# Memory is transposed un-normed, with its root applied at keys and values; its two weight slots are cut in pieces

## The reference

```python
mem_kv = (rms_norm(mem, mem_norm) @ w_mem_kv).reshape(B, M, 2, MEM_HEADS, MEM_HEAD_DIM)
mem_k, mem_v = mem_kv[:, :, 0], mem_kv[:, :, 1]
u = rms_norm(h, even_norm1[j])
q, k, v, qm = jnp.split(u @ even_w_in[j], [NA_WIDTH, 2 * NA_WIDTH, 3 * NA_WIDTH], axis=-1)
```

## Time and profile before

| what | value |
|---|---|
| median of 3 runs | 1448.41 us (1445.82 to 1448.61) |
| profiled execution, its own time | 1446.34 us |
| span of the profiled execution | 1444.1 us |
| PE busy | 1408.7 us, 98% |
| DVE busy | 1156.4 us, 80% |
| ACT busy | 974.7 us, 67% |
| mean transfer rate | 302 GB/s |

### The profile page before, as it was taken

The page is one execution under the profiler, slowest core; times in us unless marked ns, Lnnn a source line. Parts: engine busy times, 40 slices in busy tenths (PEclk is TensorE's granted clock), DMA queues, the critical chain, the costliest instruction groups (busy, mean ns, idle before and its releaser), DMA issues.

```text
span 1444.1 us, 19732 instructions
## 1 busy us (share of the span) xinstructions
PE 1408.7 (98%) x7228; PEld 1184.3 (82%) x7228; DVE 1156.4 (80%) x1013; ACT 974.7 (67%) x929; POOL 69.7 (5%) x70
## 2 busy tenths in 40 slices
PE   6999999998999999999999999999999999999997
PEld 6997888887977788888888888888888888888885
DVE  5567756664674888988888899889888889888887
ACT  6455645444853577777777777787777777777775
POOL 0000100000010300100000000000010000000000
PEclk9999999999999999999999999999999999999999
DMA  8634455544454899999999999999999999999992
GB/s 263 218 127 146 152 199 203 177 142 133 137 176 150 299 368 387 355 393 393 374 369 394 386 360 393 386 354 396 395 372 375 393 377 368 396 383 357 393 361 74
DMA packets 201942, 435.88 MB, mean 302 GB/s; under 512 B 10959, under 2 KB 41251, under 8 KB 201892
## 3 DMA queue, kind: packets, MB, share of 16 engines
q1 hardware_dynamic: 198836, 424.70, 81.1%
q0 software_dynamic: 3056, 10.50, 2.5%
HBM read 427.30 MB, written 7.88 MB: 301 GB/s over the span
## 4 chain that ended last, share of the span: by engine, by line
PE 93%; DVE 3%; ACT 2%; issue 1%; DMA 1%; POOL 0%; SPq 0%; DVEq 0%; POOLq 0%; ACTq 0%
PE ps L1583 26%; PE ps L1585 26%; PE ps L1584 26%; PE ps L1865 5%; PE ps L1867 3%; PE ps L2142 2%; DVE w_lo L1003 1%; ACT w_hi L547 1%; DMA raw<-mem_kv 1%; PE ps L1708 0%; PE ps L1672 0%; PE ps L2052 0%; PE ps L2164 0%; PE ps L1999 0%; PE ps L1686 0%
## 5 line engine op out<-in xcount | busy, mean ns | idle before, releaser
L1471 DVE TENSOR_TENSOR w_lo<-raw,w_hi 128x2048 fp32r<-128x2048 f32 (+1 forms) x221 | 436.0, 1981 | 57.0 <-ACT w_hi L847 56.7
L847 ACT ACTIVATE w_hi<-raw 128x2048 fp32r<-128x2048 f32 (+1 forms) x221 | 367.4, 1669 | 119.7 <-PE ps L1585 119.7
L1583 PE MATMUL ps<-w_hi,xt_both 128*128 128x512 f32 (+2 forms) x1048 | 405.8, 387 | 3.3 <-DVE xt_both L1364 1.5
L1585 PE MATMUL ps<-w_hi,xt_both 128*128 128x512 f32 (+2 forms) x1048 | 400.0, 382 | 0.0
L1584 PE MATMUL ps<-w_lo,xt_both 128*128 128x512 f32 (+2 forms) x1048 | 399.4, 381 | 0.0
L1471 DVE TENSOR_TENSOR w_lo<-arena,w_hi 128x2048 fp32r<-128x2048 f32 x144 | 294.8, 2052 | 27.0 <-ACT w_hi L847 26.8
L847 ACT ACTIVATE w_hi<-arena 128x2048 fp32r<-128x2048 f32 x144 | 248.8, 1728 | 82.4 <-PE ps L1585 82.4
L1583 PEld LDWEIGHTS ps<-w_hi,xt_both 128*128 128x128 f32 x1048 | 197.0, 188 | 41.1 <-issue 4.7
L1585 PEld LDWEIGHTS ps<-w_hi,xt_both 128*128 128x128 f32 x1048 | 196.9, 188 | 37.4
L1584 PEld LDWEIGHTS ps<-w_lo,xt_both 128*128 128x128 f32 x1048 | 197.2, 188 | 35.0
L1583 PE MATMUL ps<-w_hi,hT_hi 128*128 128x512 f32 x560 | 219.4, 392 | 0.0
(11 more groups left out here) (266 smaller groups left out, 1223.0 us busy)
## 6 DMA issues: line engine op xcount, KB each, us to landing
raw<-exp_gate SPq DMA_DIRECT2D x72, 1024.0 KB, 7.6
raw<-exp_up SPq DMA_DIRECT2D x48, 1024.0 KB, 8.8
arena<-exp_down SPq DMA_DIRECT2D x48, 1024.0 KB, 6.7
arena<-exp_up SPq DMA_DIRECT2D x40, 1024.0 KB, 8.4
raw<-exp_down SPq DMA_DIRECT2D x40, 1024.0 KB, 8.3
arena<-exp_gate SPq DMA_DIRECT2D x24, 1024.0 KB, 8.5
raw<-exp_up SPq DMA_DIRECT2D x32, 512.0 KB, 6.0
raw<-even_gate SPq DMA_DIRECT2D x11, 1024.0 KB, 5.3
```

What stands on the lines that cost most here:

```text
L847: ins = act.activation(w_hi[:, n % CUT, at:at + src.shape[1]], src, ACT.Copy)
L1471: ins = dve.tensor_tensor(w_lo[:, n % CUT, cols], src, w_hi[:, n % CUT, cols].bitcast(F32), ALU.subtract)
L1583: pe.matmul(dst, a[0], b[0], start=start, stop=False, skip_group_check=shared)
L1585: return pe.matmul(dst, a[1], b[0], start=False, stop=stop, skip_group_check=shared)
```

## The change

- Memory is no longer normed before its transposes: PE transposes it as it lands. Its squares are taken by ACT after x has been turned, its epsilon and root follow later (POOL takes the roots of x first; `NORM_STEP` gives the order of counts).
- The inverse root of each memory row goes to the results: values (rows on partitions) are scaled by ACT as they are copied (`mv`), keys (rows along the free dimension) are multiplied by DVE (`mkT`) with a row of roots that PE spreads over the partitions (`spread_roots0`) and ACT copies (`root0_row`). The engines of the two copies are swapped.
- Slots 0 and 1 are cut in four pieces of 512 columns each, each with its own count (`piece_hi`, `piece_lo`), and the memory projection waits for pieces in its first group. ACT does the turned copies ahead of the first pieces; DVE does half of its turned parts ahead of slot 0's pieces and half behind.
- Both halves of the memory projection come before `turn(1)`, but for the last group of the second half, which stands behind it.
- x's norm: token block 0 by ACT, block 1 by DVE.
- The first input block's first half waits for half of x's turned parts only. Ahead of its second half PE now waits for the copies of the values by ACT.
- PE multiplies zeros: 12 products of 512 columns before anything else, 6 after the memory's transposes.

```diff
+            dve.memset(hT_hi[:, 0, :].bitcast(F32), 0.0).then_inc(warm_ready, 1)   # DVE, first
 # ACT
-            act.wait_ge(mem_in, 16)
-            mean_squares(0, mem_sb, BY_TOKEN)
-            high_to(0)
+            def high_pieces(n):
+                act.wait_ge(landed[n], 16)
+                for k in range(4):
+                    cols = slice(512 * k, 512 * (k + 1))
+                    ins = act.activation(w_hi[:, n, cols], raw[:, n, cols], ACT.Copy)
+                    if k < 3:
+                        ins.then_inc(piece_hi, 1)
+                ins.then_inc(hi_ready, 1)
+                cut[0] = n + 1
             act.wait_ge(gains_ready, 1)
             turned_high(0)
+            high_pieces(0)
             act.wait_ge(x_in, 16)
             mean_squares(1, h, BY_TOKEN)
-            norm(1, h, range(TT))
+            high_pieces(1)
+            norm(1, h, range(1))
             high_to(2)
             turned_high(1)
+            act.wait_ge(turned, 8)
+            mean_squares(0, mem_sb, BY_TOKEN)
             high_to(3)
+            act.wait_ge(root0_spread, 1)
+            act.activation(root0_row, ps[:, 2, 0:T], ACT.Copy).then_inc(root0_kept, 1)
             act.wait_ge(slot_done, 2)
-            for b in range(2):
-                act.activation(mkT[:, b, :], ps[:, 4 + b, 0:T], ACT.Copy).then_inc(kv_copied_a, 1)
+            for t in range(TT):
+                act.activation(mv[:, t, :], ps[:, 6 + t, 0:256], ACT.Copy, scale=rstd[:, t:t + 1]).then_inc(kv_copied_a, 1)
 # POOL
+            inverse_root(1)
             inverse_root(0)
-            inverse_root(1)
 # DVE (low_pieces(n): the four low parts, each behind its piece_hi)
-            add_eps(0, BY_TOKEN)
-            norm(0, mem_sb, range(TT))
-            low_to(0)
-            turned_low(0)
+            turned_low(0, range(2))
+            low_pieces(0)
+            turned_low(0, range(2, 4))
             add_eps(1, BY_TOKEN)
-            low_to(1)
+            low_pieces(1)
+            norm(1, h, range(1, TT))
             low_to(2)
             turned_low(1)
+            add_eps(0, BY_TOKEN)
             low_to(3)
...
-            dve.tensor_copy(mv[:], ps[:, 6:8, 0:256]).then_inc(kv_copied_v, 1)
+            dve.wait_ge(root0_kept, 1)
+            dve.tensor_tensor(mkT[:], ps[:, 4:6, 0:T], root0_row.unsqueeze(1).broadcast_to([P, 2, T]),
+                              ALU.mult).then_inc(kv_copied_v, 1)
 # PE
+            def keep_busy(count):
+                for _ in range(count):
+                    pe.matmul(ps[:, 4, :], hT_hi[:, 0, 0:P], hT_hi[:, 0, :], start=True, stop=True)
+            pe.wait_ge(warm_ready, 1)
+            keep_busy(12)
             pe.wait_ge(early_in, 16)
...
             turn(0)
-            project(0, kv, fresh=norm_halves(0), halves=range(1), left=memory_of)
+            keep_busy(6)
+            pe.wait_ge(xt_lo_ready, 2)
+            memory_products(0)
             pe.wait_ge(xt_lo_ready, 4)
-            turn(1)
-            project(0, kv, halves=range(1, 2), left=memory_of)
+            memory_products(1)          # turn(1) stands ahead of its last group
...
             in0_block(0, 0)
-            pe.wait_ge(kv_copied_v, 1)
+            pe.wait_ge(xt_lo_ready, 8)
+            spread_roots0()             # waits rstd_ready 4; two products, the rows of roots
+            pe.wait_ge(kv_copied_a, 2)
             pe.wait_ge(rp_parts, 7)
             bias_products(0, 2)
```

More of the change, by code:

```diff
@@ L87 @@
 OUT0_BLOCKS = ((0, 1), (1, 1), (0, 0), (1, 0))
+NORM_STEP = (1, 0, 2, 3, 4, 5)
 PAIRS0 = (6, 7, 4, 5, 0, 1, 2, 3)
@@ L207, in build @@
         gnb = gain[:, 0:DV]
+        root0_row = gain[:, 768:768 + T]
         slot_pair = sb("slot_pair", [P, 2, TT, 2])
@@ L574, in norm @@
                     k = TT * i + t
-                    act.wait_ge(rstd_ready, k + 1)
+                    act.wait_ge(rstd_ready, NORM_STEP[i] * TT + t + 1)
                     for n in range(2):
@@ L1015, in add_eps @@
                     k = TT * i + t
-                    dve.wait_ge(sumsq_ready, 4 * i + pieces.index((t, 1)) + 1)
+                    dve.wait_ge(sumsq_ready, 4 * NORM_STEP[i] + pieces.index((t, 1)) + 1)
                     dve.tensor_scalar(ss[:, k, 0:1], ss[:, k, 0:1], ss[:, k, 1:2], EPS, ALU.add,
@@ L1023, in norm @@
                     k = TT * i + t
-                    dve.wait_ge(rstd_ready, k + 1)
+                    dve.wait_ge(rstd_ready, NORM_STEP[i] * TT + t + 1)
                     for n in range(2):
@@ L1034, in norm_gained, with turned_low @@
                     k = TT * i + t
-                    dve.wait_ge(rstd_ready, k + 1)
+                    dve.wait_ge(rstd_ready, NORM_STEP[i] * TT + t + 1)
                     dve.scalar_tensor_tensor(xn[:, t, cols], src[:, t, cols], rstd[:, k:k + 1], gain[:, cols],
                                              ALU.mult, ALU.mult).then_inc(xn_ready[t], 1)
-            def turned_low(i):
-                for b in range(4):
+            def turned_low(i, blocks=range(4)):
+                for b in blocks:
                     dve.wait_ge(xt_hi_ready, 4 * i + b + 1)
@@ L1106, in bias_copy, with low_pieces @@
                         ALU.add).then_inc(bias_ready, 1)
+            dve.memset(hT_hi[:, 0, :].bitcast(F32), 0.0).then_inc(warm_ready, 1)
             dve.wait_ge(gains_turned, 1)
             dve.tensor_copy(gain_of[:], ps[:, 7, 0:5 * KD]).then_inc(gains_ready, 1)
-            add_eps(0, BY_TOKEN)
-            norm(0, mem_sb, range(TT))
-            low_to(0)
+            def low_pieces(n):
+                for k in range(4):
+                    cols = slice(512 * k, 512 * (k + 1))
+                    if k < 3:
+                        dve.wait_ge(piece_hi, 3 * n + k + 1)
+                    else:
+                        dve.wait_ge(hi_ready, n + 1)
+                    ins = dve.tensor_tensor(w_lo[:, n, cols], raw[:, n, cols], w_hi[:, n, cols].bitcast(F32), ALU.subtract)
+                    if k < 3:
+                        ins.then_inc(piece_lo, 1)
+                ins.then_inc(lo_ready, 1)
+                cut[0] = n + 1
             dve.wait_ge(gains_ready, 1)
-            turned_low(0)
+            turned_low(0, range(2))
+            low_pieces(0)
+            turned_low(0, range(2, 4))
             add_eps(1, BY_TOKEN)
-            low_to(1)
+            low_pieces(1)
+            norm(1, h, range(1, TT))
             low_to(2)
             turned_low(1)
+            add_eps(0, BY_TOKEN)
             low_to(3)
@@ L1721, in _, with memory_products, spread_roots0 @@
                   + [(ps[:, 6 + t, 0:256], "by token", tok[t], slice(256, 512)) for t in range(TT)])
-            project(0, kv, fresh=norm_halves(0), halves=range(1), left=memory_of)
-            pe.wait_ge(xt_lo_ready, 4)
-            turn(1)
-            project(0, kv, halves=range(1, 2), left=memory_of)
+            def memory_products(half):
+                w = slot(half, 4)
+                for g, (dst, form, tokens, cols) in enumerate(kv):
+                    if half == 1 and g == len(kv) - 1:
+                        turn(1)
+                    for k4 in range(4):
+                        if g == 0:
+                            if k4 < 3:
+                                pe.wait_ge(piece_lo, 3 * half + k4 + 1)
+                            else:
+                                pe.wait_ge(lo_ready, half + 1)
+                        k = 4 * half + k4
+                        a, b = part(w, k4, cols), memory_of(k, tokens)
+                        if form == "by token":
+                            a, b = b, a
+                        ins = mul3(dst, a, b, k == 0, k == KD - 1)
+                ins.then_inc(slot_done, 1)
+            keep_busy(6)
+            pe.wait_ge(xt_lo_ready, 2)
+            memory_products(0)
+            pe.wait_ge(xt_lo_ready, 4)
+            memory_products(1)
+            def spread_roots0():
+                pe.wait_ge(rstd_ready, 2 * TT)
+                for t in range(TT):
+                    ins = pe.matmul(ps[:, 2, tok[t]], rstd[:, t:t + 1].broadcast_to([P, P]), ident, start=True, stop=True)
+                ins.then_inc(root0_spread, 1)
             def in0_block(b, half):
@@ L1752, in _ @@
             bias_products(4, 6)
-            pe.wait_ge(kv_copied_a, 2)
+            pe.wait_ge(kv_copied_v, 1)
             scores(0)
```

24 lines of the change are left out of this document (14 added, 10 removed).

## The result

The changed kernel takes 1451.73 us (median of 9, 1450.75 to 1453.88) against 1448.41 (median of 9, 1445.24 to 1449.30): ratio 1.0030, 95% interval 1.0022 to 1.0038. (The ratio is the record's own figure and not the quotient of the two medians, which is 1.0023; the two means differ by 4.0 us, the medians by 3.3.) The profiled execution took 1453.33, with a span of 1451.1. The forecast was 1446.2 with a range up to 1449.6: the time lies above it.

A forecast was written before the change was run, and what follows sets the result against it. PE was taken as the bound; bias products 1.2 us earlier gave 1445.1 from the profiled execution (1446.34) or 1447.2 from the median (1448.41). It predicted between them, 1446.2, range 1443.3 to 1449.6.

The forecast's parts named there:

- the zeros raising the rate: At the start: 12 zero products, 5.1 us, bring PE to the high rate by 6.3, before the memory's transposes.
- the front: Start of the kernel: PE's 16 memory transposes start near 6.7 instead of 9.38, no longer behind the memory's norm.
- the landing of the third slot: First input weights land at 21.9, unmoved by the change; the high part is done at 23.85, the low at 26.1.
- ACT's and DVE's chain behind x's turned copies: Ahead of the bias products: squares of memory, fourth slot's cut, then bias table; 11.5 us from ACT's release, ending at 35.9.
- the pause of 2 us ahead of the bias products: After the first input block's first half, PE stands about 2 us until DVE's table cut near 35.9.
- ACT could start 1.29 us after PE's start: Memory's turned copies: ACT starts them at 8.0, 1.29 us behind PE's transposes, as at the high rate.
- case A: Opening as worked out, rate held: bias products at 35.9 against 37.08, 1.2 us gained, 1445.1 us; chance 0.40.
- the first pause: Between the six extra zero products (9.6) and the first memory piece (12.35): PE stands 2.7 us.
- case B: The rate falls once in the pause before the first piece: bias start 37.6, 0.5 us slower, 1446.8; chance 0.25.
- After it nothing is late: Behind the bias start: fourth slot, bias copies and fifth slot are ready in time, so the 1.2 us gain stays.
- case C: A later pause's fall does not come, or the 2 us bias stall is absent (3.1 us gained): 1443.4; chance 0.22.
- Case D: Before 20.8: multiplying zeros does not raise the rate; bias start 39.5, 2.4 us slower, 1448.7; chance 0.13.

The follow-up runs named there:

- e1: Changed kernel with ACT's table load done early, by one 128x1 copy before its first wait: 1452.30 us, ratio 1.0024 to the kernel before.
- e4: Changed kernel without its 12 and 6 products of zeros: 1453.01 us, ratio 1.0040 to the kernel before.
- e6: Changed kernel with 16 instead of 6 products of zeros behind the memory's transposes: 1451.22 us, ratio 1.0027 to the kernel before.
- e3: Changed kernel reordered on DVE and ACT so PE has no pause ahead of the bias products: 1447.06 us, ratio 1.0001 to the kernel before.
- e10: Changed kernel with early table load, 16 instead of 6 zero products, ten products filling the bias pause, order untouched: 1447.33 us, ratio 1.0000 to the kernel before.
- e7: Kernel before with only products of zeros added, 12 at the start, 12 ahead of the memory's transposes, 18 behind: 1447.16 us, ratio 1.0000.
- e2: Changed kernel with ten unused 512-column products in PE's pause ahead of the bias products, no wait shortened: 1450.41 us, ratio 1.0018 to the kernel before.

## Why the prediction was wrong

**What held.** PE as the bound to the end; the zeros raising the rate; the front (6.44 for 6.7); pieces of DVE about 0.6 apart (2.50 for four); the landing of the third slot; ACT's and DVE's chain behind x's turned copies, 11.3 us from 26.90 to 38.20 against 11.5 in the forecast; the pause of 2 us ahead of the bias products, ended by the table's cut (2.19 and 38.05).

**The first term that failed** is "ACT could start 1.29 us after PE's start", 8.0. It did at 9.13. The table load had been hidden under a transfer, and I cost the removal of ACT's first operation without asking what stood ahead of that operation. 1.1 us at the first product; e1 takes it away in the trace. The Trainium skill says where to look: "ScalarE: Activation LUTs", section "Step-by-step: what each stage is for", has the table load placed right before the ACTIVATE that needs it. The trace agrees with that and shows that the wait of that ACTIVATE comes first; the load took 1.28 us here.

**The second** is case A itself: the rate did fall in the first pause, which was case B. The 14 products left at 0.21 cost about 1.3 us, x's transposes are 2.4 late against the forecast (25.60 for 23.2), of which 1.1 is the table. With both, the bias products are 2.3 late: 38.20 for 35.9. The prediction's own mark was that the kernel gets slower once ACT's release is later than 25.6; it came at 26.90.

**The step that decides** is "After it nothing is late". I had forecast PE's stop of 2 us ahead of the bias products, had read that after 2.08 us of idling at 433.9 the rate fell, and asked that question only of the first pause. The second pause is the worse one: in all five profiles that have it unfilled (the changed kernel twice, e1, e4, e6) it was followed by 6.8 to 6.9 us at the low rate, 3.4 us of PE's time, in a stretch where PE has no slack. The profiles' difference of 7.0 us in the span is 1.1 (the later bias products), 3.4 (this fall) and 3.4 (13.7 us low behind 60 us instead of 6.8), less 0.9 that the sum leaves over. The third term is nowhere shown to be the opening's: in the changed kernel's second profile it is missing (6.8 us low behind 60 us, as in the kernel before), so it is taken here as the luck of the first. The opening's 4.5, of which 4.3 is there at the second layer's transposes, agrees with the 4.3 us of the timed ratio (1.0030; 3.2 to 5.5 by its interval) and is more than the 3.3 between the medians; the kernel before alone wanders by more than that difference. e3 and e10, which take the fall away in two different ways, come back to the kernel before.

Two sums of the prediction are slightly off and decide nothing: case C, 1446.34 less 3.1, is 1443.2 and not 1443.4, and the upper end, 1448.7 and half of 2.1, is 1449.75 and not 1449.6.

Case C had the other half right as a mechanism (falls elsewhere come and go, at up to 1.7 us for 3.4 us low) but I gave it only the good sign. Case D, zeros that do nothing, is refuted by e7.

The Trainium skill, "TensorE: Matmul & The Clock Gate", section "Why this matters for your kernels", advises against PE-idle gaps between bursts of matmuls, but the gaps that it means are longer than this one of 2.19 us. Here the measurement decides: the shorter pause was followed by a fall in five of five profiles, and e2, the same wait filled with ten products whose results nobody uses, keeps the clock at 1.00.

## What to carry to other kernels

Before trading a pause at one place for work elsewhere, list every stop of PE that the new order makes and give each the price of a fall of its rate, here up to 3.4 us for 2.2 us of standing; a forecast pause is not free because it is short. When the first operation of an engine is removed, look at what the engine did under its wait (here the load of ACT's table) and give it something else to wait under. A gain of 1 us in a kernel like this is better read from the trace, at a mark ahead of the later falls: the bias products' start repeats within 0.5 us (37.08 and 37.55, 38.20 and 38.60), while the time wanders by 4 us and more with falls that vary between executions of the same kernel.

## What had not been expected of the hardware

Pauses of the same length and at the same place are followed by a fall in one execution and not in another (2.41 and 2.06 us around 336 to 345: none in the kernel before in both its profiles, 3.4 us in the changed one, 6.8 in e10, none in the changed kernel's second profile). Nor does a fall need one pause of 2 us: the one at 478 in the kernel before stands behind two of 0.59 and 0.76, with small products (128x8) between them. And the pause of 1.54 at 444.85, from which the prediction took that a shorter one is safe, was followed by 3.4 us at the low rate in the second profile of the same kernel (from 445.2, again behind 1.54). And no run tests the 2.19 us pause ahead of dense products instead of the 128x72 ones; that these alone don't bring the fall is shown by every run without the pause (1.65 to 1.73 us for the fourteen). The low stretches measured 3.4, 6.8 or 10.2 us. The clock's column gives 1.00 for the first 20 us of the kernel before, while its products were 0.21 us apart (the 1.2 GHz level); its record of the clock begins only at 20.85. At the start the spacing, and not that column, tells the rate.
